# Attention with the value product turned round, and head statistics summed over column groups

## The reference

```python
qa = qk_norm(heads(q_a, 8), q_gain_a) * 64 ** -0.5       # 8 heads of 64, mean of squares of each head
o_a = banded_gqa(qa, ka, va, 128, bias_a, sinks)          # 128-token window, 2 key-value groups
o_cmp, o_sel = nsa_cmp_sel(qb, k_cmp, v_cmp, k_sel, v_sel, bias_b)
o_win = banded_gqa(qb, k_win, v_win, 512, bias_b, None)
o_b = gb[..., 0, :] * o_cmp + gb[..., 1, :] * o_sel + gb[..., 2, :] * o_win
y = concat([o_a * silu(z_a), o_b * silu(z_b)])
out = x + gate * (y @ w_out)
```

## Time and profile before

| What | Value |
|---|---|
| Time, median of 3 runs | 1455.97 us (1455.06 to 1456.25) |
| Time of the profiled execution | 1455.4 us |
| Its span in the trace | 1453.7 us |
| Granted clock of TensorE over the span | 0.996 |
| PE busy | 1429.1 us of the span |
| DVE, ACT, POOL busy | 741.6, 601.9, 112.6 us |

### The profile page before, as it was taken

How to read it: one execution, slowest core, us unless ns; L and a number is a source line. 1 busy time by engine, 2 the same in 40 slices (tenths; PEclk the granted TensorE clock), 3 DMA queues, 4 the chain that set the end, 5 groups by cost and what they waited for, 6 DMA issues and landing times.

```text
span 1453.7 us, 18183 instructions
## 1 busy us (share of the span) xinstructions
PE 1429.1 (98%) x6934; PEld 1196.0 (82%) x6934; DVE 741.6 (51%) x1200; ACT 601.9 (41%) x1011; POOL 112.6 (8%) x132
## 2 busy tenths in 40 slices
PE   6999999999999999999999999999999999999998
PEld 5788889998888888888888888888888888888887
DVE  6742688855666434556455344453557333333342
ACT  5633577745333332333333445432355333333221
POOL 5302332100000000000000111100000000000000
PEclk9999999999999999999999999999999999999999
DMA  9996200113443333312213233343332333333321
GB/s 283 320 230 203 74 1 2 60 59 90 157 115 89 101 101 99 90 58 73 73 58 87 60 100 87 92 152 104 87 102 77 112 100 99 92 97 94 106 79 58
DMA packets 227825, 149.71 MB, mean 103 GB/s; under 512 B 5330, under 2 KB 216014, under 8 KB 227108
## 3 DMA queue, kind: packets, MB, share of 16 engines
q1 hardware_dynamic: 223588, 131.63, 31.1%
q0 software_dynamic: 4160, 17.04, 4.0%
HBM read 140.92 MB, written 6.68 MB: 102 GB/s over the span
## 4 chain that ended last, share of the span: by engine, by line
PE 95%; SPq 2%; DVE 1%; ACT 1%; DMA 1%; issue 1%; DVEq 0%; ACTq 0%
PE ps L435 70%; PE ps L2243 6%; PE ps L2269 3%; PE ps L1951 3%; PE ps L2168 3%; PE ps L1843 3%; PE ps L2255 1%; SPq L549 1%; SPq L579 1%; PE ps L1912 1%; PE ps L2154 1%; PE ps L2153 1%; DMA w_raw<-in_w_in_dram 1%; PE ps L1967 1%; PE ps L1974 0%
## 5 line engine op out<-in xcount | busy, mean ns | idle before, releaser
L455 DVE TENSOR_TENSOR w_lo<-w_raw,w_hi 128x1024 fp32r<-128x1024 f32 (+1 forms) x214 | 258.1, 1209 | 251.6 <-ACT w_hi L450 248.9
L450 ACT ACTIVATE w_hi<-w_raw 128x1024 fp32r<-128x1024 f32 (+1 forms) x214 | 219.5, 1034 | 15.3 <-PE ps L435 11.3
L501 ACT ACTIVATE temps<-ps 128x512 f32<-128x512 f32 x67 | 40.0, 596 | 238.8 <-PE ps L435 238.8
L435 PE MATMUL ps<-g_hi,w_hi 128*128 128x512 f32 x384 | 95.8, 392 | 0.0
L435 PE MATMUL ps<-g_hi,w_lo 128*128 128x512 f32 x384 | 94.9, 389 | 0.0
L435 PE MATMUL ps<-g_lo,w_hi 128*128 128x512 f32 x384 | 94.8, 389 | 0.0
L435 PEld LDWEIGHTS ps<-g_hi,w_lo 128*128 128x128 f32 x384 | 72.1, 188 | 15.1
L435 PEld LDWEIGHTS ps<-g_lo,w_hi 128*128 128x128 f32 x384 | 72.1, 188 | 14.9
L435 PEld LDWEIGHTS ps<-g_hi,w_hi 128*128 128x128 f32 x384 | 71.5, 188 | 14.6
L435 PE MATMUL ps<-f_lo,w_hi 128*128 128x512 f32 x288 | 71.1, 389 | 0.0
L435 PE MATMUL ps<-f_hi,w_hi 128*128 128x512 f32 x288 | 71.1, 389 | 0.0
(11 more groups left out here) (446 smaller groups left out, 2750.4 us busy)
## 6 DMA issues: line engine op xcount, KB each, us to landing
w_raw<-in_w_in_dram SPq DMA_DIRECT2D x107, 512.0 KB, 3.9
w_raw<-in_w_ff_gate_dram SPq DMA_DIRECT2D x22, 512.0 KB, 3.8
w_raw<-in_w_ff_up_dram SPq DMA_DIRECT2D x22, 512.0 KB, 3.8
w_ada_shift_scale<-in_w_ada_dram SPq DMA_DIRECT2D x16, 512.0 KB, 8.1
w_raw<-in_w_r_out_dram SPq DMA_DIRECT2D x16, 512.0 KB, 4.5
w_raw<-in_w_ff_down_dram SPq DMA_DIRECT2D x16, 512.0 KB, 4.1
w_ada_gate<-in_w_ada_dram SPq DMA_DIRECT2D x4, 1024.0 KB, 11.1
x_spill<-x_t POOLq DMA_DIRECT2D x2, 2048.0 KB, 8.5
```

The costliest lines, as they stand in the source:

```text
L435: mm = pe.matmul(bank, w[:, slot, k], mov[:, at_k], start=first and n == 0 and k == 0, stop=last and n == 2 and k == kts - 1)
L450: act.activation(whi[:, slot, 0:kts], raw[:, slot, 0:kts], ACT.Copy).then_inc(hi_done, 1)
L455: nc.vector.tensor_tensor(wlo[:, slot, 0:kts], raw[:, slot, 0:kts], whi[:, slot, 0:kts].bitcast(F32), ALU.subtract).then_inc(lo_done, 1)
L501: act.activation(dst, ps[:, o % 4], func, scale=scale).then_inc(evac, 1)
```

## The change

Attention is now driven by pairs n of two heads (48 pairs) instead of single steps; heads are taken in their natural order. In iteration n PE writes the scores of both heads of pair n, multiplies the values by the probabilities of pair n - 2, and transposes both heads of pair n - 1. The value product is turned: the 64 value columns of a key block are stationary, 128 columns of transposed probabilities stream past, and the two heads of the pair write the lower and the upper 64 partitions of the same PSUM bank. A narrow pair (1 or 2 key blocks) has both heads in one transposed bank and one copy, by DVE for even pairs and ACT for odd ones; a wide pair (3 or 4 blocks) has a copy by each. The result has head dimensions on the partitions and needs no turning for the output product; its coefficients do: POOL widens them to 128 x 512 (`widen`), PE turns them by 4 transposes a group (`coefficients_wide`), ACT copies them out, and DVE multiplies (`combined`). The gate multiplication moves from DVE to POOL (`y_gate`). There are four score buffers. The compressed probabilities are normalised by POOL and transposed inside attention (iteration 3) instead of before it, and the compressed product is 16 matmuls of 128 columns.

The head statistics are turned as well: 32 columns of `half_sel` are stationary, the 512 tokens of squares stream past, and up to four tiles write four groups of 32 partitions of one bank; ACT copies the bank and PE turns it by 4 transposes. The first weights of the output product after the third unit are loaded only after attention, since the raw weight buffer holds transposed probabilities meanwhile.

```diff
-STATS_IN = {(16, 1): (0, 1), (17, 0): (2,), (17, 1): (3,), (17, 2): (4, 5), (18, 0): (6,), (18, 1): (7,), (18, 2): (8,),
-            (19, 0): (9,), (19, 1): (10,)}
+STATS_AT = {(16, 1): 0, (17, 1): 1, (18, 1): 2}
+TURN_AT = {(17, 0): 0, (18, 0): 1, (19, 0): 2}
...
+CTR_AT = 3
+CO_PE_AT = (5, 6, 7, 9)
+K_WINDOW_AT = (2, 3, 4, 4)
...
+PAIRS = N_ATT // 2
+COEF_AT = (8,) + tuple(range(10, PAIRS, 4))
...
+                if k == 3:
+                    sp.wait_ge(m["pv_mm"], PAIRS)
...
+            g.tensor_tensor(csc_heads, csc_heads,
+                            cden[:].rearrange("p g q -> p (g q)").unsqueeze(2).to_broadcast([P, 32, NC_PAD]),
+                            ALU.mult).then_inc(m["cpool_done"], 1)
...
+            def widen(G):
+
+                pool.wait_ge(m["cf_done"], G + 1)
...
+                g.tensor_copy(wide_of(G).rearrange("p t (h d) -> p t h d", h=2),
+                              coef[:, G % 2].rearrange("p (t h) -> p t h", h=2).unsqueeze(3).to_broadcast([P, 4, 2, HD])
+                              ).then_inc(m["cpool_done"], 1)
...
+            for n in range(PAIRS + 2):
+                if n - 1 in COEF_AT:
+                    G = COEF_AT.index(n - 1)
+                    act.wait_ge(m["aux_tr"], G + 3)
...
+                    a.activation(coef_wide(G), ps[:, 6], ACT.Copy).then_inc(m["aux_ev"], 1)
+                if n < PAIRS:
+                    exponential(2 * n)
+                    exponential(2 * n + 1)
...
+                p = n - 1
+                if 0 <= p < PAIRS and (wide_pair(p) or p % 2):
+                    act.wait_ge(m["t_mm"], 2 * p + 2)
...
+                    a.activation(dst[:, 0:w], ps[:, 3, 0:w], ACT.Copy).then_inc(m["pt_a"], 1)
...
+            for n in range(PAIRS + 2):
+                if n < PAIRS:
+                    biased(2 * n)
+                    biased(2 * n + 1)
+                p = n - 1
+                if 0 <= p < PAIRS and (wide_pair(p) or p % 2 == 0):
+                    dve.wait_ge(m["t_mm"], 2 * p + (1 if wide_pair(p) else 2))
...
+                    v.tensor_copy(pt_of(2 * p)[:, 0:w], ps[:, 2, 0:w]).then_inc(m["pt_d"], 1)
...
+                if n - 1 in CO_PE_AT:
+                    compressed_branch(CO_PE_AT.index(n - 1))
...
+                if n >= 5 and (n - 5) % 4 == 0 and n < PAIRS:
+                    coefficients((n - 5) // 4)
...
+                if n - 1 in COEF_AT:
+                    combined(COEF_AT.index(n - 1))
...
-                for i in range(NI):
-                    mm = pe.matmul(ps[:, 4, 8 * t + 2 * i:8 * t + 2 * i + 2], proj[:, 20 + t % 4, blk(i)], half_sel[:],
+                for t in range(a, b):
+                    pe.wait_ge(m["sq_done"], t + 1)
+                    mm = pe.matmul(ps[32 * (t - a):32 * (t - a) + 32, 4], half_sel[:], proj[:, 20 + t % 4],
                                    start=True, stop=True)
...
-                    for b in range(blocks):
-                        c = (u.first_block + b) * P + u.g * HD
-                        mm = pe.matmul(ps[:, 4 + u.group % 2, u.head * HD:(u.head + 1) * HD], pt[:, t % 2, blk(b)],
-                                       proj[:, v, c:c + HD], start=b == 0, stop=b == blocks - 1)
...
+                for b in range(blocks):
+                    c = (u.first_block + b) * P + u.g * HD
+                    for half in range(2):
+                        mm = pe.matmul(ps[half * HD:half * HD + HD, 4 + u.group % 2, blk(n % 4)], proj[:, v, c:c + HD],
+                                       pt_of(2 * n + half)[:, blk(b)] if wide_pair(n) else pt_of(2 * n)[:, blk(half * blocks + b)],
+                                       start=b == 0, stop=b == blocks - 1)
...
+            def coefficients_wide(G):
+
+                pe.wait_ge(m["cpool_done"], G + 3)
...
+            for n in range(PAIRS + 1):
+                if n < PAIRS:
+                    scored(2 * n)
+                    scored(2 * n + 1)
+                if n == 0:
+                    v_local()
+                if n >= 2:
+                    weighted(n - 2)
+                if n >= 1:
+                    transposed(2 * n - 2)
+                    transposed(2 * n - 1)
+                if n == CTR_AT:
+                    compressed_transposed()
+                if n in CO_PE_AT:
+                    compressed_out(CO_PE_AT.index(n))
+                if n in COEF_AT:
+                    coefficients_wide(COEF_AT.index(n))
+            early_out(0)
+            weighted(PAIRS - 1)
+            coefficients_wide(N_GROUPS - 1)
```

More of the change, by code:

```diff
@@ L132, in __init__, with wide_pair, copies @@
         self.first_block = self.i + 1 - blocks
+def wide_pair(p):
+    return Step(2 * p).width > 2 * P
+def copies(p, engine):
+    return sum(wide_pair(n) or n % 2 == engine for n in range(p + 1))
 def norm_group(t):
@@ L141, in att @@
     return Step(s)
-def tails_at(s):
-    return [(i, half) for i in range(NI) for half in range(2)
-            if s == (24 * i + 29 + 3 * half if i < NI - 1 else 24 * i + 13 + 17 * half)]
 class Own:
@@ L779, in add_branch @@
                     pool.wait_ge(m["co_done"], i + 1)
[L780 to L784 removed]
+                else:
                     pool.wait_ge(m["ob_done"], 2 * i + 1)
@@ new lines, in coefficients @@
+            def coefficients(G):
+                i, branch = divmod(G, 3)
+                cf, dn = coef[:, G % 2], den[:, G % 2]
+                dve.wait_ge(m["s_exp"], 8 * G + 8)
+                if branch == 0:
+                    dve.wait_ge(m["sinkexp_done"], i + 1)
+                    own(v.tensor_tensor(dn, dn, sink_exp[:], ALU.add))
+                    own.wait()
+                if G >= 2:
+                    dve.wait_ge(m["aux_tr"], G + 1)
+                if branch == 0:
+                    v.reciprocal(cf, dn).then_inc(m["cf_done"], 1)
+                    return
+                own(v.reciprocal(cf, dn))
+                own.wait()
+                v.tensor_tensor(cf, cf, gate_of(branch)[:, i], ALU.mult).then_inc(m["cf_done"], 1)
@@ new lines, in transposed @@
+            def transposed(t):
+                p, half = divmod(t, 2)
+                w = att(t).width
+                pe.wait_ge(m["s_exp"], t + 1)
+                before = p - 1 if wide_pair(p) or wide_pair(max(p - 1, 0)) else p - 2
+                if half == 0 and before >= 0:
+                    for engine, name in enumerate(("pt_d", "pt_a")):
+                        if copies(before, engine):
+                            pe.wait_ge(m[name], copies(before, engine))
+                for b in range(w // P):
+                    bank, c = (2 + half, b) if wide_pair(p) else (2 + p % 2, half * w // P + b)
+                    mm = trans(ps[:, bank, blk(c)], sc_of(t)[:, blk(b)])
+                mm.then_inc(m["t_mm"], 1)
@@ new lines, in weighted @@
+            def weighted(n):
+                u = att(2 * n)
+                for engine, name in enumerate(("pt_d", "pt_a")):
+                    if wide_pair(n) or n % 2 == engine:
+                        pe.wait_ge(m[name], copies(n, engine))
+                if n == 0:
+                    pe.wait_ge(m["vt_ev"], 3)
+                elif n % 4 == 0 and u.group >= 2:
+                    pe.wait_ge(m["comb_done"], u.group - 1)
+                v, blocks = (VA, VS, VW)[u.branch], u.width // P
+                for b in range(blocks):
[4 more added lines that the diff above has]
+                                       start=b == 0, stop=b == blocks - 1)
+                mm.then_inc(m["pv_mm"], 1)
```

503 lines of the change are left out of this document (256 added, 247 removed).

## The result

| | Before | After |
|---|---|---|
| Median (lowest to highest) of 6 executions each | 1455.59 us (1454.87 to 1456.25) | 1461.81 us (1460.03 to 1463.35) |
| Profiled execution, its span | 1455.4, 1453.7 us | 1461.94, 1460.2 us |

The changed kernel is slower: the ratio is 1.0042, with a 95% interval of 1.003 to 1.0055, so 6.2 us. The forecast was 1457.0 with a range of 1446 to 1464: the time lies in the range, but 0.8 us above the part of it that I gave to my own likeliest case (1453 to 1461). I had given faster 0.37, no change 0.29 and slower 0.34; it came out slower.

What follows compares the result with a forecast made beforehand. PE, busy 98% of the span, was taken to bound the kernel. Attention's +6.35 us and the statistics' -5.0 on 1455.4 gave 1456.8 for the profiled execution, stated as 1457 us, range 1446 to 1464.

Steps and rivals of the forecast that it cites:

- my own likeliest case: Whole kernel: attention's loss and the statistics' gain nearly cancel, 1453 to 1461 us; chance 0.45.
- path of an iteration: Attention: product waits for the copy after the last transposes; cycle 1.34 us for 1 block, 2.02 for 2.
- Statistics and the eight transposes ahead of attention: Before attention: four column groups at once, 1.2 us a call, gain 5.0 us; eight transposes leaving, -0.75.
- 12 pairs of 1 block: Attention's first window: 24.9 us against 20.1, +4.8, with slow filling, compressed products, coefficients and key rounding.
- 20 pairs of 2 blocks: Attention: five groups of 8.9 us against 7.9 before, +5.0 us.
- 8 pairs of 3 blocks: Attention: 9.9 us a group and 1.0 for weight conversions, 20.8 us for both as before, so 0.
- 8 pairs of 4 blocks and what trails them: End of attention: shorter iterations -3.2, turned coefficients +0.9, output's last transposes gone -0.4: -2.7 us.
- the change of shape: Around each turned value product: emptying and uncovered loads cost 0.3 us an iteration, 48 times, 14.4 us.
- the first iterations fill slowly: Start of attention: slow filling, and iteration 3's eight transposes wait for POOL's product: 2.4 us.
- no gap on PE at the output units: Output units after attention: a sign that PE would show no gap there.
- Faster: Attention: engines keep ahead and PE's own work counts, -7 us, -12 with statistics; 1443, likelier 1447; chance 0.30.
- Slower: Groups of 1 and 2 blocks: POOL's widened coefficients late, PE waits 1 us more in six groups, 1463; chance 0.16.

Runs made afterwards that it cites:

- a faster copy: Changed kernel with pairs of 2 blocks copied by head, DVE one and ACT the other at once: 1456.38 us.
- the gaps filled: Changed kernel plus ten identity transposes ahead of pair 2's scores and ten ahead of the first compressed product: 1459.95 us.
- transposes first: Changed kernel with a narrow pair's two transposes ahead of the product of the pair before it, instead of behind: 1454.08 us.
- the kernel with the statistics alone: Kernel before with nothing but the new head statistics, POOL's queue order unchanged: 1456.74 us, ratio 1.0011.
- the later-gates kernel: Changed kernel with DVE's gate and compressed-coefficient work and the turned compressed probabilities one iteration later, compressed products in 6, 7, 9, 11: 1461.7 us.

## Why the prediction came out as it did

The path of an iteration, the sizes of the 2-block groups and the statistics held; three terms came out too small, all on the slow side, 5.5 us together. The time stayed in the range because the range was wide enough for them, not because I had priced them. Prediction and measurement by its own terms, in us:

| Term | Predicted | Measured |
|---|---|---|
| Statistics and the eight transposes ahead of attention | -5.75 | -5.7 |
| Start of the first z pass, which differs from execution to execution | 0 | -0.5 |
| 12 pairs of 1 block | +4.8 | +7.6 |
| 20 pairs of 2 blocks | +5.0 | +5.0 |
| 8 pairs of 3 blocks | 0 | +1.7 |
| 8 pairs of 4 blocks and what trails them | -2.7 | -1.7 |
| Sum | +1.35 | +6.4 |

**Right: the path of an iteration.** Groups of 2 blocks were to take 8.9 us and took 8.33, 8.87, 8.91, 9.44 and 8.99. That the product waits for a copy was shown twice: a faster copy gave 5.4 us, an order in which the copy has more to hide in 7.7. Before a product of 2 blocks the weight loads stood 0.32 to 0.97 us, where I had said 0.6. The longer ones belong to ACT, whose copy stands behind two exponentials; I had 0.4 a group for that.

**Right, in part by luck: the statistics,** 1.1 us a call for 1.2 predicted, four column groups at once, and a gain of 4.9 for 5.0. Two errors cancel in it. I had read the 1.82 us of the earlier trace rows as that of 16 statistics instructions, but it is the spacing of the pass ahead of them; they take 1.70 (124.26 to 125.96), and by their starts all 88 took 9.2 us and not 9.9. The new calls and transposes took 4.3 and not 4.9. The figure of the Trainium skill for three column tiles (TensorE: Matmul & The Clock Gate, Part 3), by which the gain would have been 4.3, was too cautious for four tiles: a call of eight instructions took 1.09 us, two slots of 0.43 and the two changes of shape. And the term was right only because the diff holds another edit, POOL's queue, which neither my description of the change nor my prediction has. Without it the gain is nothing.

**Right in kind, too high in size: the change of shape,** 0.23 us for an in-and-out where PE sets the pace, for 0.3. The halves run at once: eight product instructions take 0.66 us in the timeline and sixteen 1.09, so 0.11 for each two.

**The term that failed: the 12 pairs of 1 block,** "together 24.9". At full clock, with the gaps filled, they took 25.0, in the changed kernel 27.7. The rest is the clock, which my sum held at 1.0: the earlier trace rows show 1.00 with PE busy 17.7 of 20.1 us, and the change took PE to long empty stretches in just this place. That 24.9 and 25.0 agree so well is luck in part. The two stalls (1.2 for DVE's gates, 1.0 for ACT's copy) I had as part of "the first iterations fill slowly" and as the rounding of keys; the third compressed product waited 1.1 us, where my 3.75 leaves it 0.2 (32 instructions of 0.11 are 3.5); and POOL, which I expected to hold PE in iteration 3, didn't.

**The second: 3 blocks, "0".** My 9.9 a group and 1.0 for the conversions, 20.8 in all, would have been off by 0.4 without the collision of POOL's gate product and DVE's conversion; apart, the two groups take 21.2, and 22.5 with it. The change moved the gate product to POOL, and I had priced it as POOL's time only, with nobody to wait for it. The Trainium skill has this as a rule (SBUF — State Buffer, section "SBUF: two separate sides"): DVE with two operands in SBUF and a POOL operation that reads SBUF hold one port pair in turn, the later one waiting. The trace agrees: POOL ended at 271.40, and DVE's operation ended 1.08 us after that.

**The third: "no gap on PE at the output units".** There is one of 0.9, for the last lower half of the output. Without it the 4-block part would be at -2.6, and the term was -2.7. The chain is coefficients, widening, transposes, copy, two multiplications, a sum and the remainder; I followed none of it past the last product.

**The rivals.** "Faster" (the engines keep ahead) fell as the change is written. With transposes first PE does wait for almost nobody in the 2-block groups, but they come out 1.6 us below before and not 7 (20 pairs of 0.35, less some 2 for the coefficients): PE's own work in them was more than this rival had. "Slower" by POOL's widening gave a time (1463) close to the measured one by a cause that isn't there: a widening took 0.61 us, not 1.01, and PE waited for none in the changed kernel.

**What stays open.** Why the clock falls in one execution and not in another of the same code with the same waits. How much of the median is owed to it can only be estimated: the mean granted clock is 0.9945 over the six executions of the changed kernel and 0.9963 over 22 of the kernel before, and 0.0018 of 1460 us is 2.6 of the 6.2 us, if PE sets the pace. Executions whose code is the same up to attention also came to it at 193.3 to 194.7 us. That difference is there at the first z pass already (120.0 to 121.4), and from it to attention all ten traces with the changed attention have 73.3 us; where in the first 120 us it arises was not followed.

## What to carry to other kernels

When an operation is moved nearer to the one that feeds it, compute the path from the last input through the copy to its use, and try the other order of the two independent pieces between them first: here swapping transposes and product was worth 7.7 us and no instruction. Price a stage in which PE gets gaps at half clock too, not only at full. When work goes to another engine, look at what else it shares with its neighbour, and at each queue that a shortened stage now catches up with.

## What the runs showed of the hardware

- TensorE's granted clock went to half (1.2 of 2.4 GHz) from 199.4 to 202.8 and from 206.2 to 209.6 us, behind stalls of 1.2 and 1.0 us in a stretch of 27.7 us in which PE was busy 23.0. The same code kept 1.00 in one execution and had 0.85 over a window of 23.5 us in another, where the longest wait before the fall was 0.6 us. With twenty useless transposes in the gaps, the one traced execution kept 1.00 and its 12 pairs were 2.7 us shorter. In the kernel with the statistics alone one wait of 4.2 us was followed by half clock from 148.5 to 151.9 us.
- DVE's operation on 96 columns with one input (L1541) took 1.15 us in the changed kernel and ended at 196.16, as POOL's work did (196.10); with POOL idle, in the later-gates kernel, it took 0.20. The conversion of 1024 columns took 2.33 beside POOL's product and 1.22 apart. DVE's biases and copies, which read PSUM, kept their 0.55 beside POOL's work from 268.89 to 270.17.
- Four column groups of 32 write one PSUM bank at once, in float32 and with 512 columns: 1.09 us for eight instructions and both changes of shape.
- Changing the array's shape and back cost 0.23 us between matmuls of 128 columns (0.91 for four), and 0.23 around the 512 columns of a statistics call (1.09 less two slots of 0.43).
